# A two-layer hybrid mixer on one core: products of ones ahead of the first projection, transposes of probabilities in pairs, square roots kept in PSUM, and one low part moved

## The reference, cut to what matters

```python
def reference(x, norm_mix, w_in, ...):          # x: 1 x 256 x 1024, float32, DEPTH = 2
    for i in range(DEPTH):
        h = rmsnorm(x, norm_mix[i])
        x = x + token_mixer(h, w_in[i], ...)
        x = x + peer(rmsnorm(x, norm_ffn[i]), peer_wq[i], peer_keys[i], peer_u[i], peer_v[i])
    return rmsnorm(x, norm_final)

def token_mixer(h, w_in, ...):
    c = split_columns(h @ w_in)
    o_ret = retention(c['ret_q'], c['ret_k'], c['ret_v'], c['ret_g'], ret_norm)   # rmsnorm by head of 64
    o_moba = moba(rope(c['moba_q']), rope(c['moba_k']), c['moba_v'])
    o_ssm = mamba2(c['ssm_z'], c['ssm_xbc'], c['ssm_dt'], ...)                    # rmsnorm by group of 128
    o_nsa = nsa(rope(c['nsa_q']), ...)           # compressed, selected and window attention, gated
    return concatenate([o_ret, o_moba, o_ssm, o_nsa]) @ w_out
```

## Time and profile before

| | |
|---|---|
| median of 3 runs | 1925.31 us (1924.02 to 1925.44) |
| the profiled execution's own time | 1925.47 us |
| its span | 1923.7 us |
| VectorE busy | 1299.8 us (68%) |
| GpSimd busy | 1247.1 us (65%) |
| ScalarE busy | 996.7 us (52%) |
| mean busy share of the DMA engines | 53% |
| granted TensorE clock, mean | 0.997 |

### The profile page before, as it was taken

One profiled execution on the slowest core, in us unless ns is written; L12 is line 12 of the kernel. 1 busy time (PEld: TensorE's weight loads), 2 busy tenths in 40 slices (PEclk: granted clock), 3 DMA queues, 4 the chain that ended last, 5 costly groups with the idle time before them and its releaser, 6 DMA issues. The chain is left out here.

```text
span 1923.7 us, 38013 instructions
## 1 busy us (share of the span) xinstructions
PE 1907.7 (99%) x12350; PEld 1698.5 (88%) x12350; DVE 1299.8 (68%) x2922; ACT 996.7 (52%) x1581; POOL 1247.1 (65%) x626
## 2 busy tenths in 40 slices
PE   9999999999999999999999999999999999999998
PEld 9898888899999888888898888888999998888886
DVE  5666799789997444444466658996999964444444
ACT  5654544655444455455466554447554445445444
POOL 6447788877776555555574487888767765555553
PEclk9999999999999999999999999999999999999999
DMA  6525555554445665666545355555444455555553
GB/s 222 181 96 174 187 190 189 186 166 154 160 156 164 195 193 191 194 192 191 184 165 182 101 173 197 186 185 186 165 154 159 157 173 191 193 195 192 191 196 131
DMA packets 93240, 338.40 MB, mean 176 GB/s; under 512 B 10352, under 2 KB 10736, under 8 KB 93168
## 3 DMA queue, kind: packets, MB, share of 16 engines
q1 hardware_dynamic: 93168, 337.54, 53.2%
HBM read 336.45 MB, written 1.05 MB: 175 GB/s over the span
## 5 line engine op out<-in xcount | busy, mean ns | idle before, releaser
L491 POOL TENSOR_TENSOR WL<-ring,WH 128x1024 fp32r<-128x1024 f32 x360 | 869.4, 2419 | 334.6 <-ACT WH L1417 174.2
L1417 ACT CAST WH<-ring 128x1024 fp32r<-128x1024 f32 x512 | 538.3, 1052 | 695.0 <-PE PS L1110 329.4
L520 POOL TENSOR_TENSOR HX<-G,HX 128x256 fp32r<-128x256 f32 x256 | 371.8, 1453 | 320.6 <-ACT HX L1526 320.6
L2150 DVE TENSOR_TENSOR WL<-ring,WH 128x1024 fp32r<-128x1024 f32 x248 | 303.9, 1225 | 370.9 <-ACT WH L1417 370.9
L1110 PE MATMUL PS<-WH,HX 128*128 128x512 f32 x2048 | 506.2, 389 | 0.0
L1110 PEld LDWEIGHTS PS<-WH,HX 128*128 128x128 f32 x2048 | 384.3, 188 | 79.7
L1000 PE MATMUL PS<-HX,WH 128*128 128x512 f32 x1248 | 313.2, 393 | 0.0
L1110 PE MATMUL PS<-WL,HX 128*128 128x512 f32 x1024 | 274.0, 389 | 0.0
L1000 PEld LDWEIGHTS PS<-HX,WH 128*128 128x128 f32 x1248 | 224.5, 189 | 40.3
L1042 PE MATMUL PS<-HX,WH 128*128 128x256 f32 x1024 | 255.9, 288 | 0.0
L1043 PE MATMUL PS<-HX,WH 128*128 128x256 f32 x1024 | 250.6, 283 | 0.0
(11 more groups left out here) (262 smaller groups left out, 2091.0 us busy)
## 6 DMA issues: line engine op xcount, KB each, us to landing
ring<-stream SPq DMA_DIRECT2D x636, 512.0 KB, 3.3
X<-x_t SPq DMA_DIRECT2D x4, 256.0 KB, 4.0
out_t<-X SPq DMA_DIRECT2D x2, 512.0 KB, 2.7
CN<-consts SPq DMA_DIRECT2D x1, 851.0 KB, 9.7
WF<-last SPq DMA_DIRECT2D x1, 512.0 KB, 10.2
PR<-params SPq DMA_DIRECT2D x2, 239.0 KB, 4.9
CN<-consts SPq DMA_DIRECT2D x1, 64.0 KB, 3.9
```

The costliest lines, as they stand in the source:

```text
L491: nc.gpsimd.tensor_tensor(WL[:, b, :], ring[:, slot, :], WH[:, b, :].bitcast(F32), ALU.subtract).then_inc(done, 1)
L520: nc.gpsimd.tensor_tensor(GL[:, s, :], G[:, tile, :], GH[:, s, :].bitcast(F32), ALU.subtract).then_inc(L.gl_ready, 1)
L1417: nc.scalar.copy(WH[:, b, :], ring[:, slot, :]).then_inc(L.hi_ready, 1)
L2150: V.tensor_tensor(WL[:, s % 2, :], ring[:, (U0 + s) % SLOTS, :], WH[:, s % 2, :].bitcast(F32), ALU.subtract).then_inc(L.vlo_ready, 1)
```

## The change

Four edits.

In layer 0, TensorE gets more products of ones, with results that nobody reads, in PSUM bank 2: three ahead of the wait for x's third part, one ahead of the wait for the fourth, nine ahead of the first projection.

The turns of window and selected attention are made in pairs of heads: on TensorE, with `project(13, (1,))` between the pairs of the first group and `compress(6)` between those of the second; on ScalarE, the copies of the first group's heads 2 and 3 move behind the cast of projection 14's first piece and the exponentials of heads 2 and 3 of the second group. ScalarE still copies the second group's four heads in one go.

The two Newton steps write their last result to PSUM, where the scaling multiplies then read it.

On VectorE, `lower_m(2)` moves from behind the second root's mean to ahead of the square and the sum that make it.

```diff
-        gvar, grs = small(4), small(4)
+        gvar = small(4)
         rrs_ps, grs_ps = PS[:, 7, 0:8], PS[:, 7, 8:12]
-        rvar, rrs, gnt, rroot, groot = (small(8) for _ in range(5))
+        rvar, gnt, rroot, groot = (small(8) for _ in range(4))
...
                     for t in range(TT):
                         if layer == 0:
+                            spin(bank[2][:, 0:P], 3 if t == 0 else 1)
                             pe.wait_ge(x_in[2 + t], 16)
...
+                    if layer == 0:
+                        spin(bank[2][:, 0:P], 9)
                     first_unit()
...
                     compress(4)
-                    turn_group(SC4[0], 0)
+                    turn_group(SC4[0], 0, (0, 1))
                     project(13, (1,))
+                    turn_group(SC4[0], 0, (2, 3))
                     compress(5)
                     project(14, (0,))
-                    turn_group(SC4[1], 1)
+                    turn_group(SC4[1], 1, (0, 1))
                     compress(6)
+                    turn_group(SC4[1], 1, (2, 3))
...
-                    def probabilities(buf):
-                        for h in range(NH):
+                    def probabilities(buf, heads=range(NH)):
+                        for h in heads:
                             taken(buf[:, h, :], 384).then_inc(L.tr_evac, 1)
...
                     exps(1, SC4[1], (0, 1))
-                    probabilities(PT[0])
+                    probabilities(PT[0], (0, 1))
                     upper(2 * PROJ.index(14))
                     exps(1, SC4[1], (2, 3))
+                    probabilities(PT[0], (2, 3))
                     take(13, next_too=False)
                     act.wait_ge(L.seg_ready, 4)
                     nc.scalar.activation(SEG[:, :, :], SEG[:, :, :], ACT.Exp).then_inc(seg_exp, 1)
...
-                    step(newton_ps(rvar, rroot, rrs_ps, gnt, rrs))
-                    V.tensor_tensor(m_part(0), heads(ra), columns(rrs), ALU.mult).then_inc(L.m_ready, 1)
+                    step(newton_ps(rvar, rroot, rrs_ps, gnt, rrs_ps))
+                    V.tensor_tensor(m_part(0), heads(ra), columns(rrs_ps), ALU.mult).then_inc(L.m_ready, 1)
 
                     lower_m(1)
                     step(V.tensor_tensor(ya, ya, TB[:, 512:1024].rearrange("p (t n) -> p t n", t=TT), ALU.mult))
+                    lower_m(2)
                     step(V.tensor_tensor(yb.rearrange("p (t n) -> p t n", t=TT), ya, ya, ALU.mult))
                     step(V.tensor_reduce(gvar, yb.rearrange("p (k n) -> p k n", n=P), AX.X, ALU.add))
                     V.tensor_scalar(gvar, gvar, 1.0 / P, EPS, ALU.mult, ALU.add).then_inc(L.g_var, 1)
-                    lower_m(2)
                     dve.wait_ge(g_rs, 2 * layer + 2)
-                    step(newton_ps(gvar, groot[:, 0:4], grs_ps, gnt[:, 0:4], grs))
+                    step(newton_ps(gvar, groot[:, 0:4], grs_ps, gnt[:, 0:4], grs_ps))
...
-                                    bc(grs.rearrange("p (t g) -> p t g", t=TT), 3, P), ALU.mult).then_inc(L.m_ready, 1)
+                                    bc(grs_ps.rearrange("p (t g) -> p t g", t=TT), 3, P), ALU.mult).then_inc(L.m_ready, 1)
```

## The result

The changed kernel takes **1935.79 us** (median of 6 runs, 1930.26 to 1939.84) against 1924.20 for the kernel before in the same session (6 runs, 1923.49 to 1925.44): a ratio of 1.0056, interval 1.0046 to 1.0067. It is slower by 0.6%, 11.6 us, where I had forecast +0.5 us. The profiled execution took 1936.59 us, with a span of 1934.8.

A forecast was written before the change was run, and what follows sets the result against it. TensorE was taken to bound the kernel, busy 1907.7 of 1923.7 us. The parts' -1.5 + 3.4 - 1.4 = +0.5 us, put on the median of 1925.31, gave 1925.8 us, range 1921.0 to 1928.9.

The forecast's parts named there:

- Part 1, the ones: Start of layer 0: products of ones keep the clock up through the 3.41 us half-speed stretch, -1.5 us.
- The rival: Start of layer 0: ones among transposes do not hold the clock, the 1.5 us comes back, 1927.3; chance 0.06.
- Part 2, turns in pairs: Window and selected attention, both layers: waits on copies go, but VectorE's later queue costs 1.7 us each, +3.4.
- group one: First group's turns of heads: TensorE's 0.55 us wait for ScalarE's copy goes.
- Group two: Second group's turns: 0.49 us wait goes; exponential 0.76 later, leaving 0.61 of TensorE's 1.04 us wait.
- The queue: VectorE's rotary group, both layers: two GpSimd subtractions alternate with VectorE multiplies, delaying the addition; 1925.8, chance 0.52.
- The stall: Ahead of the window products, each layer: TensorE idle 2.3 us waiting for VectorE's addition.
- Part 3, roots: End of the mixer: scaling multiply about 0.69 us, TensorE's low products 0.72 earlier in each layer, -1.4 us.
- the slower rival: Window products, each layer: clock falls behind the new stalls, costing 1.5 to 1.7 each, up to 1929.2; chance 0.12.
- the 2.01 that I had named as the point: Idle time at the start behind which the clock fell; a stall as long decides for the clock's fall.

The follow-up runs named there:

- four and six copies: Kernel before plus four or six extra VectorE copies of 512 columns ahead of the addition the window products wait for: 1935.37 us (four), 1940.81 us (six).
- pairs alone: Kernel before with only the turns in pairs of heads: 1935.27 us, ratio 1.0062.
- roots alone: Kernel before with only the roots in PSUM and the third pair's low part moved: 1923.65 us, ratio 0.9994.
- three copies: Kernel before plus three extra VectorE copies of 512 columns ahead of the addition the window products wait for: 1927.10 us, ratio 1.0017.
- copies moved without ones: Changed kernel with ScalarE's copies of the first group's heads 2 and 3 behind the large exponential, without the products of ones: 1922.24 us, ratio 0.9990.
- copies moved: Changed kernel with ScalarE's copies of the first group's heads 2 and 3 moved behind the large exponential: 1922.10 us, ratio 0.9989.
- the later spread: Kernel before with the products of ones and the query stage's four spreading products (diagonal times ones) issued one step later: 1923.62 us, ratio 0.9994.
- two removals: Changed kernel with GpSimd's second subtraction held until VectorE's addition: 1922.94 us; or with ScalarE's copies of heads 2 and 3 behind the large exponential: 1922.10 us.
- the stall filled: Changed kernel with ten products of ones ahead of the window products in both layers, where TensorE waits for VectorE's addition: 1928.19 us, ratio 1.0019.
- a stall of its own making: Kernel before with six, four or three extra VectorE copies of 512 columns ahead of the addition: 1940.81, 1935.37, 1927.10 us.

## Why the prediction was wrong

**Part 1, the ones.** In the profiled execution right: the clock is at 1.00 from 4.99 us on, the first weight product starts at 11.12 (11.03), and -1.38 of the -1.5 arrives. The rival took up what the Trainium skill ("TensorE: Matmul & The Clock Gate", Part 4, PE-mode transpose) says of transposes, that they do not count as busy in the way products do; the clock fell there in none of the seven profiles with ones, but in only three of seven without them, so these runs do not bear on that rule much. What the step missed is that the low stretch of 3.41 us belonged to that one execution: of seven profiles without ones it is in three (the kernel before, four and six copies) and not in four (pairs alone, roots alone, three copies, copies moved without ones), and what sets them apart is small: the three waited 1.9 to 2.2 us for the first weights and 0.6 to 0.8 in all for x, the four 1.7 to 1.8 and 0.2 to 0.4. That points to the first DMAs, whose time differs between executions. I made the sum against one execution and put it on the median as if the median had that stretch. In medians the ones are worth 0.1 us (copies moved, with and without them) to 0.7 (with the later spread, against the kernel before, so the spread's share is in it); alone they measured 1.8 slower, by the wait at the query stage.

**Part 2, turns in pairs.** The waits of L649 on ScalarE are gone and group one gives 0.58 (I said 0.55). Group two gives nothing in layer 0: the exponential stands at 88.85, which against TensorE's shift of -1.38 is 1.02 later, not 0.76, since the cast ahead of it waits for its DMA, and that moved by only 1.11 (85.78 to 84.67). TensorE still waits 0.54 there. The queue then formed as worked out, in layer 1 at the very two instructions named (L1666 and L1667 of the kernel before), in layer 0 one sooner. The stall is 2.21 and 2.07 where 2.3 was forecast, and the net of the part without the clock is (-0.58 + 0.32 + 2.28) + (-0.58 + 2.14) = +3.58, against +3.4. That the two are so close is in part luck: layer 0 lost 2.02 and layer 1 lost 1.56, where 1.7 was forecast for each.

**Part 3, roots.** 0.69 and 0.69 us for the two scalings (I said 0.69), and -0.69 and -0.74 on TensorE where -0.72 twice was forecast.

**The step that failed** is the price and the chance of the slower rival: "The price is 1.5 by the stretch at the start, up to 1.7 if dense products fill 3.41 us at half speed", with 0.12, and "against it, dense products lie on both sides of these". Everything else sums to -1.38 + 3.58 - 1.43 + 0.05 = +0.82 against my +0.5; the clock adds 4.68 and 4.72. Both halves of the step were wrong. Even the rival's own sum came to 1929.2 at most, 6.6 us under the measured 1935.79. Size: I took the one low stretch that the trace showed for the length of any, and it was three times as long, 10.24. At the start the products of 256 columns were running when the clock was low; here it is 24 records of 64 columns, 8 of 15 columns and 8 of transposes, and the clock returned only with projection products running again, after 1.6 us of those in layer 0 and 4.0 in layer 1. Chance: waits of 1.56 and 1.45 us were enough at this place, so mine, longer than the 2.01 that I had named as the point, made the fall the likely case and not a rival of one in eight. That dense products on both sides would hold the clock was argued from nothing that the trace showed, and they do not lie on both sides: directly behind the stall stand the narrow ones. At the query stage, where wide products do follow, the clock fell once and held once. (The Trainium skill, "TensorE: Matmul & The Clock Gate", "Why this matters for your kernels", warns only of idle gaps longer than the 1.45 to 2.21 us behind which the clock fell here; by that rule it would have held, and the measurement decides.)

Shown: that the pairs carry the loss (each part run alone), that the copies' place makes the stall and GpSimd's second subtraction is needed for it (two removals), and that the fall of the clock behind it is 7.6 of the loss (the stall filled). The kernel before with a stall of its own making shows the same fall, so none of the change's other edits is needed for it. Not shown: why the low stretch lasts 6.8 us in one place and 13.7 in another, whether the narrow products make it longer, and what decides between a fall and none behind equal waits.

## What to carry to other kernels

When an edit puts a new idle time of a microsecond or two into a TensorE-bound kernel, do not price it as the stall alone: carry a fall of the clock behind it as a case with a real chance, and do not take its length from one other stretch of the trace. Here 2.1 us of waiting cost 6.9, and where a wait could not be taken out, products of ones in it took the fall away. Before taking waiting instructions off one engine, list what stands behind the moved ones on the other engine, and who shares its SBUF port next: here a small multiply that came 0.1 us too late waited for a whole subtraction of GpSimd. And where a kernel's executions differ, a gain read off one profile (a low stretch that goes away) is worth only its share of executions.

## What the runs showed of the hardware that was not expected

- The clock's low stretches in the middle of the kernel lasted 6.82 to 13.65 us, with TensorE busy for all or nearly all of them (10.24 of 10.24, in the changed kernel's layer 1), around stalls of 1.45 to 3.0 us ahead of the window products. Behind 0.90 us the clock did not fall in the one execution seen. At the query stage, ahead of wide products, a wait of 2.83 us was followed by no fall in one execution and by 3.41 us at half speed in another.
- At the start the clock fell, for 3.41 us only, in the three profiles without ones that waited 1.9 to 2.2 us for the first weights, and stayed up in the four that waited 1.7 to 1.8. The wait for x differed as well (0.6 to 0.8 against 0.2 to 0.4), so which of the two mattered is not shown; a few tenths of a microsecond that differ from one execution to the next went with a fall or none.
- A VectorE instruction of 128 columns that takes 0.29 us by itself took 2.52 behind a GpSimd subtraction, and with TensorE waiting for it the executions of one kernel lay 3 to 5 us apart (1923.6 and 1926.5 to 1928.8). With the waiting products one step later they did not.
